# Products for the row maxima of the global heads: full-height, or in pairs on two halves of the array

## The reference, cut to what matters

```python
q = rmsnorm(q, gq).transpose(0, 2, 1, 3)
k = rmsnorm(k, gk).transpose(0, 2, 1, 3)
...
s = jnp.einsum('bkgqd,bksd->bkgqs', qblk, k).astype(jnp.float32) * scale
p = jax.nn.softmax(s, axis=-1).astype(v.dtype)
return jnp.einsum('bkgqs,bksd->bkgqd', p, v)
```

## Time and profile before

| what | us |
|---|---|
| median of 3 runs | 2790.13 (2788.76 to 2790.58) |
| the profiled execution | 2787.31 |
| its span, first to last instruction | 2785.5 |
| `attend_global` in it | 360 to 1071 |
| busy in the span: PE, DVE, ACT, POOL | 2596.2, 1905.9, 1398.9, 1003.3 |

### The profile page before, as it was taken

The page is one execution under the profiler, slowest core; times in us unless marked ns, Lnnn a source line. Parts: engine busy times, 40 slices in busy tenths (PEclk is TensorE's granted clock), DMA queues, the critical chain, the costliest instruction groups (busy, mean ns, idle before and its releaser), DMA issues. The chain is left out here.

```text
span 2785.5 us, 34506 instructions
## 1 busy us (share of the span) xinstructions
PE 2596.2 (93%) x11730; PEld 2103.9 (76%) x11730; DVE 1905.9 (68%) x2461; ACT 1398.9 (50%) x2082; POOL 1003.3 (36%) x720
## 2 busy tenths in 40 slices
PE   7999875999999997998996999989997999999997
PEld 5888744777777776787775888868885888888886
DVE  5565564999999986785556777777775435455566
ACT  3333244887888886783334444444443332323342
POOL 1111154989898996560000333323323000000011
PEclk9999977999999998999998999989998999999998
DMA  5333334111222103633663444554444445436465
GB/s 172 105 100 107 101 89 72 36 32 30 61 58 54 31 20 93 176 95 119 200 210 106 151 144 162 175 180 166 151 142 169 166 147 194 157 130 219 147 225 206
DMA packets 281299, 355.08 MB, mean 127 GB/s; under 512 B 41811, under 2 KB 191443, under 8 KB 280116
## 3 DMA queue, kind: packets, MB, share of 16 engines
q1 hardware_dynamic: 262848, 337.67, 39.1%
q10 hardware_dynamic: 16756, 12.25, 1.6%
q0 software_dynamic: 1536, 3.15, 0.4%
HBM read 223.55 MB, written 117.83 MB: 123 GB/s over the span
## 5 line engine op out<-in xcount | busy, mean ns | idle before, releaser
L687 POOL TENSOR_TENSOR p_sum<-p_sum,p_hi 128x1024 f32<-128x1024 f32 x160 | 383.5, 2397 | 31.2 <-issue 16.8
L108 PE MATMUL u_pr<-u_t_hi,u_w_hi 128*128 128x512 f32 x896 | 352.8, 394 | 32.1 <-DVE u_t_lo L1680 32.1
L108 PE MATMUL d_pr<-d_w_hi,d_s_hi 128*128 128x512 f32 x896 | 350.4, 391 | 28.4 <-DVE d_s_lo L1935 28.4
L109 PE MATMUL u_pr<-u_t_lo,u_w_hi 128*128 128x512 f32 x896 | 351.8, 393 | 0.0
L110 PE MATMUL u_pr<-u_t_hi,u_w_lo 128*128 128x512 f32 x896 | 351.7, 392 | 0.0
L109 PE MATMUL d_pr<-d_w_lo,d_s_hi 128*128 128x512 f32 x896 | 350.0, 391 | 0.0
L110 PE MATMUL d_pr<-d_w_hi,d_s_lo 128*128 128x512 f32 x896 | 349.7, 390 | 0.0
L719 ACT ACTIVATE p_hi<-s_ps 128x1024 fp32r<-128x1024 f32 x256 | 263.7, 1030 | 165.5 <-PE s_ps L814 165.5
L751 DVE TENSOR_REDUCE part_max<-m_ps 128x1 f32<-128x1024 f32 x251 | 305.6, 1217 | 52.1 <-PE m_ps L796 51.8
L765 DVE TENSOR_TENSOR p_lo<-s_ps,p_hi 128x1024 fp32r<-128x1024 f32 x256 | 313.5, 1224 | 39.8 <-ACT s_ps L720 35.5
L720 ACT ACTIVATE s_ps<-s_ps 128x1024 f32<-128x1024 f32 x256 | 262.1, 1024 | 0.0
(11 more groups left out here) (226 smaller groups left out, 5651.3 us busy)
## 6 DMA issues: line engine op xcount, KB each, us to landing
d_s_lo<-act_blocks SPq DMA_DIRECT2D x112, 512.0 KB, 3.8
act_blocks<-u_s_out SPq DMA_DIRECT2D x128, 256.0 KB, 6.4
d_w_raw<-in_w_ffn_down SPq DMA_DIRECT2D x112, 256.0 KB, 3.9
act_blocks<-u_a_sum SPq DMA_DIRECT2D x96, 256.0 KB, 2.4
u_w_first<-in_w_ffn_up SPq DMA_DIRECT2D x16, 1024.0 KB, 6.1
u_w_raw<-in_w_ffn_up SPq DMA_DIRECT2D x16, 1024.0 KB, 6.1
x_in<-in_x SPq DMA_DIRECT2D x16, 512.0 KB, 4.4
q_turned<-w_raw SPq DMA_DIRECT2D x16, 512.0 KB, 3.3
```

Source lines behind the costliest of these rows:

```text
L108: nc.tensor.matmul(out, stat_hi, mov_hi, start=first, stop=False)
L109: nc.tensor.matmul(out, stat_hi, mov_lo, start=False, stop=False)
L687: nc.gpsimd.tensor_tensor(p_sum[:, s], first, p_hi[:, (UNITS * n + u) % SLOTS].bitcast(F32), ALU.add).then_inc(added, 1)
```

## The change

The two products of a pair no longer run over 128 rows. The first contracts rows 0 to 63, with the queries' high parts from `q_max`; the second contracts rows 64 to 127, with the queries' high parts from `q_all`. The keys' operand is cut to the same rows. The maxima are then those of high of q times high of k. Loads, waits, banks, columns and counts of instructions stay.

```diff
+                q_high = (q_max[0:HD], q_all[HD:2 * HD])
                 for e in range(2):
-                    last = nc.tensor.matmul(bank[:, e], q_all[:, n % QS, t * P:(t + 1) * P],
-                                            kt[:, n // ITER, 0, (c + e) * NB:(c + e + 1) * NB], start=True, stop=True)
+                    last = nc.tensor.matmul(bank[:, e], q_high[e][:, n % QS, t * P:(t + 1) * P],
+                                            kt[e * HD:(e + 1) * HD, n // ITER, 0, (c + e) * NB:(c + e + 1) * NB], start=True, stop=True)
                 last.then_inc(max_product, 1)
```

## The result

| | before | changed |
|---|---|---|
| median, us | 2789.45 | 2816.64 |
| lowest to highest, 4 runs each | 2788.24 to 2790.58 | 2816.49 to 2821.40 |
| span of the profiled execution | 2785.5 | 2814.8 |

A forecast was written before the change was run, and what follows sets the result against it. PE was taken to bound `attend_global`. Savings of 17.1 us over 27.6 iterations plus 1.2 ahead of the first scores, less 1 at the end, gave 17: profiled 2770.3, median 2773 us, range 2768 to 2793.

The forecast's parts named there:

- What bounds the kernel: In `attend_global` PE sets the pace, needing 19.97 of an iteration's 20.27 us; DVE's sum 18.61, POOL's floor 19.53.
- the forecast's sum for PE: Per iteration, eight units 18.64, two L831 products 0.47, L843 0.86: 19.97 us, all but 0.30 of it.
- A pair's time on PE: Pair of products for maxima: between 0.47 and 0.23 us; 0.25 taken, saving 0.22 a pair, 1.76 an iteration.
- the lower one: The bound with a pair's two products side by side on PE: 0.23 us for both.
- The rival on the other side: Array emptied at each change of height around a pair, 0.17 us each; iteration 21.1, time 2812 us; chance 0.13.
- What is late next: With PE at 18.2 us, DVE (19.55) and POOL (19.53) limit the iteration: 19.65 us, saving 0.62.
- Ahead of the first scores: Three pairs in a chain of product and reduce before the first scores; 0.4 us saved each, 1.2 in all.
- the stage's end: At the end of the stage POOL still has its last additions to do and takes about 1 us back.
- Clock: No change forecast: it was 1.00 in the stage's last 22 us, where PE had fewer products.
- the 0.86 of `total`: L843's share of PE's time in an iteration: 731.18 - 730.09 less one product, 0.86 us.

The follow-up runs named there:

- pairs twice: The changed kernel with each pair of half-height products issued twice, four between two changes of height; 2876.71 us, ratio 1.0315.

## Why the prediction was wrong, point by point

- *What bounds the kernel.* Right. PE set the pace: one more product in a unit, 0.233 x 8 = 1.86 us, made the iteration with 96 rows longer by about 1.45 (21.72; maxima at 493.16 and 1079.50). The other 0.41 went into waits that PE had; the forecast's sum for PE had left 0.30 for them. One fewer made it shorter.
- *A pair's time on PE.* Of the two bounds the lower one was right: the products start together, and "TensorE: Matmul & The Clock Gate", Part 3, of the Trainium skill, which has them 4 ns apart, agrees with the trace (0.00 to 0.01).
- **The step that failed** is the one behind it: "A pair then saves 0.22 us and an iteration 8 x 0.22 = 1.76". It priced the two changes of height at nothing. They cost 0.20 us each: (2.50 - 2.33 + 0.23) / 2, of which about 0.10 is the later start of the load and about 0.11 the load itself, which is in the open (a product right behind a border is recorded 0.50 long instead of 0.39). Two of them make 0.40, against the 0.23 saved, so the pair lost 0.17 us where it was to save 0.22.
- *Why it was dismissed.* The earlier trace rows show changes of width at no cost, and the prediction let them stand for changes of height. The experiments show that width and 96 rows are indeed free and 64 rows are not. The Trainium skill's rule in "TensorEngine Tiling (Array Packing)", Key Properties, that a change of tiling mode drains TensorE, agrees with the trace for height (the load starts 0.33 us after the last product instead of with it); with these shapes a change of width showed nothing of the kind (0.23). The rule was quoted and its rival given a chance of 0.13.
- *The rival on the other side* had the right mechanism and the right order: 0.17 a change where 0.20 was measured, the iteration 21.1 for 21.26, 2812 us for 2816.6. That it came so near is partly luck: its price took the shown end of a product for the moment at which the next may start, 0.07 more than the 0.10 measured, and left out the 0.11 of the load that is no longer hidden. It named 0.11 a change as the point from which it decides.
- *What is late next.* Nearly right, and tested by itself: 19.76 us for 19.65, DVE's idle time 0.90 us for 0.94. The time was 2777.1 for 2773, which is 11.7 us less than the kernel before took beside it (2788.8), where 17 was forecast. 27 iterations account for 13.8 in the profile; the 1 us for the stage's end was not measured by itself.
- *Ahead of the first scores.* Right in size: 1.3 us at the first scores for 1.2, and 1.2 in the changed kernel (379.18), where it is gone by the first row maximum (394.93 for 393.95).
- *Clock.* The forecast had none of it, see the last section: some 3 us of the 27.

## What to carry to other kernels

Two half-height products side by side cost one, but going to half height and back costs 0.40 us with products of 512 columns, as much as 1.7 of them; no other number of columns was run. One pair between two borders loses 0.17 us. An estimate from the same numbers: in place of full-height ones two pairs would win 2 x 0.23 - 0.40 = 0.06 and three 0.29; no run has such a kernel. So gather such products where nothing else stands between them, or leave them alone. Here `m_ps` has room for one pair and DVE must empty it first, so they can't be gathered as the kernel is built. And look at the weight loads before and after an edit on PE: a load that no longer starts with the product before it is the sign of a border, and here about half of its price. An analogy from one kind of change (width) to another (height) needs a run.

## What the runs showed that was not expected

- What counts isn't fewer rows than the neighbour: products over 65 and 96 rows between full ones come at 0.23 us, one over 64 rows costs two borders. Fewer than 64 rows were not run.
- A break of the same size was in the kernel before all along, without a change of height. Behind L843, the product that the profile shows as two, L813 is recorded 0.79 long, and the L814 after it starts 0.63 us later, 0.40 more than usual:

```profile
730.55 0.79 PE L813 MATMUL s_ps<-q_all,kt 128*128 128x512 f32 x1
```

  The forecast had that time in its sum (in the 0.86 of `total`) and did not ask where it comes from. L843 is the only product of the stage's loop whose operands are not `F32R`; whether that is the reason no run here tests.
- After the long stop PE runs at the lower clock for a while. In the kernel before, products were spaced at full speed again from 476.67, 4.1 us after the stop's end; in the changed kernel from 484.85, 10.7 us after it. By windows, 470 to 480 and 480 to 490 us, first the kernel before, then the changed one (PE, PEld, DVE, ACT, POOL busy, then granted clock):

```profile
470.00:480.00 10.00, 7.45 (x25) 5.98 (x26) 3.78 (x4) 4.13 (x5) 7.64 (x5) 0.69 0.28 62
480.00:490.00 10.00, 10.00 (x42) 7.54 (x41) 9.18 (x9) 7.85 (x10) 9.30 (x5) 1.00 0.07 14
```

```profile
470.00:480.00 10.00, 5.89 (x14) 3.93 (x14) 2.45 (x2) 1.94 (x2) 6.24 (x4) 0.50 0.36 76
480.00:490.00 10.00, 10.00 (x33) 6.50 (x32) 6.03 (x5) 7.02 (x8) 7.84 (x5) 0.75 0.06 14
```

The clock was 0.50 (1.2 GHz) and 0.75 in the changed kernel, where it was 0.69 and 1.00; 0.69 and 0.75 are means of stretches with both levels. That this is due to the half-height products is not shown: with the extra product over 96 rows it lasted 6.6 us, with pairs twice 5.9, with both products on rows 0 to 63 6.3, so two of the kernels with half-height products are no longer in it than one without. What it hangs on stays open; it is 3 us once and doesn't touch the iterations, in which the clock is 1.00.
